# Gates of a hybrid diffusion layer: operand parts ahead of taking the product out of its bank

## The reference

```
h = rms_norm(x, norm1_w) * (1 + sc1) + sh1
proj = h @ w_in
hy, qkv, scv, gates = split(proj)
ya, yb, yc = hyena(hy), attention(qkv), short_conv(scv)
ga, gb, gc = split(gates, 3)            # 3 x 1024 columns
merged = sigmoid(ga)*(ya @ w_br_a) + sigmoid(gb)*(yb @ w_br_b) + sigmoid(gc)*(yc @ w_br_c)
x = x + g1 * (merged @ w_o)
```

## Time and profile before

| what | value |
|---|---|
| median of 3 executions | 2281.6 us (2279.53 to 2285.46) |
| the profiled execution's own time | 2278.91 us |
| its span, first to last instruction | 2277.1 us |
| mean granted TensorE clock | 0.975 |
| PE busy, share of the span | 94% |
| VectorE and ScalarE busy | 72% and 47% |
| gates of layer 0 | from 229.66 to 386.14 us |
| gates of layer 1 | from 1283.84 to 1440.26 us |

### The profile page before, as it was taken

The page is one execution under the profiler, slowest core; times in us unless marked ns, Lnnn a source line. Parts: engine busy times, 40 slices in busy tenths (PEclk is TensorE's granted clock), DMA queues, the critical chain, the costliest instruction groups (busy, mean ns, idle before and its releaser), DMA issues.

```text
span 2277.1 us, 34993 instructions
## 1 busy us (share of the span) xinstructions
PE 2138.9 (94%) x13094; PEld 1715.0 (75%) x13094; DVE 1630.9 (72%) x2405; ACT 1073.0 (47%) x1636; POOL 158.6 (7%) x176
## 2 busy tenths in 40 slices
PE   7998999999998997899998999999989999699999
PEld 2448999999656995566666999999765998466665
DVE  4857776654768646899997677663668654699997
ACT  2433444322712223788884444322451223588885
POOL 1010000000000100111110000000000100011110
PEclk8999999999999999899999999999999999799999
DMA  9772233212323423999993233322404431799997
GB/s 369 258 268 100 109 132 139 71 65 82 114 92 113 164 88 145 365 380 382 388 391 111 86 127 126 116 63 72 158 11 157 142 130 56 287 384 385 381 377 275
DMA packets 75656, 436.32 MB, mean 192 GB/s; under 512 B 8905, under 2 KB 9545, under 8 KB 34618
## 3 DMA queue, kind: packets, MB, share of 16 engines
q1 hardware_dynamic: 52896, 347.63, 39.7%
q0 software_dynamic: 18320, 72.87, 10.3%
q10 hardware_dynamic: 4300, 13.90, 1.8%
HBM read 384.87 MB, written 49.50 MB: 191 GB/s over the span
## 4 chain that ended last, share of the span: by engine, by line
PE 66%; DVE 15%; ACT 6%; issue 5%; DVEq 4%; DMA 3%; ACTq 0%; POOL 0%; POOLq 0%
PE ps L658 27%; PE ps L1173 9%; PE ps L1199 5%; PE ps L1177 4%; PE ps L831 3%; PE ps L885 3%; PE ps L1203 2%; DVE back L1918 2%; PE ps L757 2%; DVE front_r L1902 2%; PE ps L739 2%; PE ps L950 2%; ACT front_r L1267 2%; PE ps L697 1%; DVE back L1963 1%
## 5 line engine op out<-in xcount | busy, mean ns | idle before, releaser
L658 PE MATMUL ps<-front_r 128*128 128x320 f32 x3584 | 589.7, 311 | 12.2 <-DVE back_r L2194 8.4
L658 PEld LDWEIGHTS ps<-front_r 128*128 128x128 f32 x3584 | 542.3, 189 | 14.3 <-DVE front_r L1699 9.7
L1267 ACT ACTIVATE front_r<-ring 128x1024 fp32r<-128x1024 f32 (+1 forms) x204 | 184.9, 907 | 337.6 <-PE ps L658 256.0
L1267 ACT ACTIVATE back<-ps 128x512 f32<-128x512 f32 (+5 forms) x200 | 98.2, 507 | 375.1 <-PE ps L658 174.0
L1699 DVE TENSOR_TENSOR front_r<-ring,front_r 128x1024 fp32r<-128x1024 f32 x100 | 122.3, 1224 | 157.6 <-ACT front_r L1267 156.5
L885 PE MATMUL ps<-back_r,front_r 128*128 128x320 f32 x1152 | 176.7, 309 | 0.0
L885 PEld LDWEIGHTS ps<-back_r,front_r 128*128 128x128 f32 x1152 | 170.9, 188 | 0.0
L2288 DVE TENSOR_TENSOR back_r<-front,back_r 128x1024 fp32r<-128x1024 f32 x128 | 153.4, 1219 | 5.0 <-ACT back_r L1267 3.4
L1173 PE MATMUL ps<-back_r 128*80 128x512 f32 x384 | 152.0, 396 | 3.7 <-ACT back_r L1267 3.7
L1173 PE MATMUL ps<-back_r,front_r 128*80 128x512 f32 x384 | 151.9, 396 | 0.0
L658 PE MATMUL ps<-back_r,front_r 128*128 128x320 f32 x640 | 147.6, 312 | 0.0
(11 more groups left out here) (269 smaller groups left out, 3630.7 us busy)
## 6 DMA issues: line engine op xcount, KB each, us to landing
ring<-in_stream SPq DMA_DIRECT2D x186, 1024.0 KB, 6.5
front<-in_stream SPq DMA_DIRECT2D x80, 1024.0 KB, 18.0
back<-in_stream SPq DMA_DIRECT2D x48, 1024.0 KB, 18.9
gates<-back SPq DMA_DIRECT2D x24, 640.0 KB, 3.1
back<-gates POOLq DMA_DIRECT2D x48, 320.0 KB, 3.3
kspec<-back POOLq DMA_DIRECT2D x20, 512.0 KB, 7.0
front<-kspec POOLq DMA_DIRECT2D x4, 2048.0 KB, 10.8
rows<-front ACTq DMA_DIRECT2D x10, 520.0 KB, 2.7
```

Of the source, the lines that this page charges most:

```text
L658: mm = pe.matmul(tokh(b)[:, c0:c1], w(wp)[:, k, :], src(hp, k)[:, c0:c1], start=first, stop=last)
L1267: return act.activation(o, i, ACT.Copy)
```

## The change

In a step of the gates both engines turn round two pieces of work: the part of the operand of product n + 4 is made first, and product n is taken out of its bank second. What is waited for, the tiles, the banks and the instructions themselves are as before.

```
--- before.py
+++ after.py
@@ -1444,9 +1444,9 @@
                 operand_hi(2)
                 operand_hi(3)
                 for n in range(PRODUCTS):
-                    gate_taken(n)
                     if n + 4 < PRODUCTS:
                         operand_hi(n + 4)
+                    gate_taken(n)
                     if n == 7 * (N_GATE - 1):
                         act.wait_ge(qs_ready, l + 1)
                         act.activation(st5[:], st5[:], ACT.Sqrt, bias=eps[:, 0:1], scale=1.0 / HD).then_inc(qrt, 1)
@@ -2002,9 +2002,9 @@
                     operand_lo(n)
                 for n in range(PRODUCTS):
                     g, j = n // 7, n % 7
-                    gate_sum(n)
                     if n + 4 < PRODUCTS:
                         operand_lo(n + 4)
+                    gate_sum(n)
                     if j == 0:
                         weight_sum(g, 3)
                     elif j == 2 and g + 1 < N_GATE:
```

## The result

The changed kernel takes 2305.3 us (median of 4 executions, 2301.88 to 2306.52), the kernel before 2280.57 us beside it (2276.12 to 2285.46). The ratio is 1.0109, 95% interval 1.0095 to 1.0123. 2303.7 us was forecast. The change costs 24.7 us against the median beside it, where 22.1 us was forecast; that the two times lie only 1.6 us apart is in part luck, since the base stood 1.0 us lower this time. The profiled execution took 2305.6 us, its span is 2303.8 us.

The account below looks back on a forecast made before the run. PE was taken to bound the gates, apart from bank waits. Eleven waits of each kind, 1.77 us a pair, made each stage 167.5 us, the two 22.1 us longer: 2281.6 + 22.1 = 2303.7 us, range 2294 to 2312.

Parts of the forecast that it names:

- What bounds the gates: Gates: PE sets the pace at 1.76 us a product, losing 0.74 us a group waiting for VectorE to release bank 4.
- What the change takes away: Gates: VectorE's 1.87 us wait for the operand behind the sigmoid goes; alone, at most PE's 8.5 us a layer gained.
- The wait ahead of product 6: Gates, each group: product 6 waits 0.53 us for VectorE's sum of product 4, now behind an operand (4.05 against 3.52 us).
- The wait ahead of product 2: Gates, each group: product 2 newly waits 1.24 us for ScalarE's copy of product 0, through a chain across both engines.
- 12.32 + 0.53 + 1.24: Gates: group time without waits plus the waits ahead of products 6 and 2, giving 14.09 us a group, previously 13.06.
- the prediction's lower bound: Gates: if weight sum 2 held nobody, ScalarE would start 0.30 us earlier, 6.6 us less in all, 2297 us.
- Only the wait for bank 4: Rival, gates: the copy of product 0 is in time; 153.9 us a stage, 2276.4 us in all; chance 0.05.
- All waits gone: Rival, gates: no PE waits remain; 148.03 us a stage, 16.8 us less in all, 2264.8 us; chance 0.04.
- given back behind the stage: Rival, experts: DMA transfers start as early as now, so later computation recovers the gates' loss; 2281.6 us; chance 0.04.
- The fourth rival: Gates: the clock falls in the new gaps for a quarter of products, 59 us more, 2363 us; chance 0.03.
- settled into a cycle: Gates: the cycle repeats each group; a rival had waits growing instead, above 2312 us, chance 0.04.
- SP's store: SP's queue: gate store about 1.4 us later, next load not before some 13 us on; costed at nothing.

Follow-up runs that it names:

- ScalarE's half alone: Kernel before, with only ScalarE making the operand first and VectorE in its old order: 2264.82 us, ratio 0.9929.
- step 6 on ScalarE: Kernel before, with ScalarE making the operand first only in the step where the sigmoid L1426 stands: 2264.06 us, ratio 0.9933.
- The sum of product 4 first: Changed kernel, but VectorE sums product 4 ahead of the operand's low part, as before: 2308.59 us, ratio 1.0117.
- the copy first: Changed kernel, but ScalarE copies product 0 out of its bank ahead of the operand, as before: 2293.64 us, ratio 1.0054.
- the weight sum earlier: Changed kernel, but VectorE makes the next group's weight sum 2 ahead of the sum of product 5: 2297.96 us, ratio 1.0082.
- the sum of product 6 first: Changed kernel, but VectorE sums product 6 ahead of the operand's low part, as before: 2277.62 us, ratio 0.9986.
- VectorE's half without step 6: Kernel before, with only VectorE making the operand's low part first, except where it sums product 6: 2304.6 us, ratio 1.0108.

## Why the prediction was right, point by point

**What bounds the gates.** PE does, but for the release of a bank. Confirmed from the other side: with no wait (ScalarE's half alone) the stage is 148.14 us, and 148.03 was worked out from the pitch of 1.76 us.

**What the change takes away.** "The wait of 1.87 us goes": with ScalarE's half alone VectorE waits 0.17 us for that operand. In the changed kernel the wait doesn't go but is split: 0.76 us for the same operand (302.56), and 1.14 us for the next one (305.71), which is now the one behind the sigmoid. VectorE has caught up before the sum of product 4 even so: it waits 0.25 us for the operand ahead of that sum. One link of the change (step 6 on ScalarE) is worth 16 us, measured alone (2264.06 against 2280.2 us). The change had a gain in it, and gave it back and more.

**The wait ahead of product 6.** 0.53 us forecast, 0.53 measured, and the new cause as said: in the earlier trace rows the sum of product 4 was late because VectorE was behind, after the change because it stands behind a low part. The chain that ended last shows it, link by link, from the end of product 4's matmuls:

```profile
311.69 0.64 ACT front_r L1267
312.33 0.02 issue
312.36 0.69 DVE front_r L1902
...
313.14 0.50 DVE back L1918
313.64 0.04 issue
313.69 5.55 PE ps L885 x36
```

**The wait ahead of product 2.** 1.24 us forecast, 1.34 measured. From the start of product 6 (299.59, with the 0.10 by which its row is early) the links are: sum of product 5 at 1.12 (1.12 forecast), weight sum 2 at 1.53 (1.53), operand at 2.30 (2.26), low part at 2.97 (2.93), sum of product 6 at 3.75 (3.71), sigmoid at 4.27 (4.24), operand at 5.46 (5.41), copy from 5.99 to 6.41 (5.95 to 6.37). PE then went on 0.21 us after the copy had ended, not 0.15. These hundredths are the 0.10 us a group, 2.2 of the 2.8 us by which the stages came out longer than 167.5 each; another 0.28 in each layer is a single longer gap of ScalarE's, ahead of its operands at 333.70 and 1427.22 (0.45 us instead of 0.17).

**Where the working was right only in its sum.** The prediction added "12.32 + 0.53 + 1.24" as two costs. The sum of product 4 first shows that they aren't: the 14.19 us stay when the 0.53 are gone. The prediction's own links say so, had they been read to the end: product 5 stood "0.53 + 1.76" ahead of product 6, so whatever is taken from the 0.53 comes on top of the 1.24. What sets the group is one loop: from product 2 three products to the start of product 5, and from its end through both helpers (operand, low part, sum, weight sum, operand, low part, sum, sigmoid, operand, copy) back to the next product 2. Each link inside it counts in full or to the point where another takes over: the copy first takes 0.54 us off, the weight sum earlier 0.34 (the prediction's lower bound had 0.30 for this and 2297 us; 2297.96 was measured). The wait ahead of product 6 lies beside it, and costs only when the loop is broken, as with the sum of product 6 first.

**The rivals.** "Only the wait for bank 4" gave 153.9 us for a stage; the kernel that breaks the loop in step 6 has 154.07. "All waits gone" gave 2264.8 us; ScalarE's half alone has 2264.82. Both were the right price for a condition that the change as a whole doesn't meet. Nothing clear of the spread was given back behind the stage: the 24.85 us of the two stages are the 24.7 us of the medians. In the changed kernel's profile the clock stayed at 1.00 in both stages, with two pauses in each group and none longer than 1.39 us, so the rule of the Trainium skill on cycling through banks ("TensorE: Matmul & The Clock Gate", section "A second HAM failure mode: psum-queue depth-cycling") didn't come to bear on it. The fourth rival is not empty for all that: with the sum of product 4 first, and with VectorE's half without step 6, the clock fell once in one of the two stages, behind pauses of 1.92 and 1.77 us, and cost about 1.5 us each time. It was far from the quarter of all products that the rival's price supposed. The waits settled into a cycle at once: 14.18 and 14.19 us, group after group, but for the one longer gap of ScalarE's in each layer.

**SP's store.** Costed at nothing, with about 1.4 us of delay: the sigmoid ends 5.28 us after the start of product 6 instead of 3.86. The distance in the prediction was wrong, which changed nothing: the next load of SP's queue doesn't start some 13 us on but 6.0 us behind the store (316.08 and 310.03) before the change, and 5.8 us behind it (310.71 and 304.94) after it. In both kernels SP waits for PE there, and PE waits for no landing in any of the rows above.

## What to carry to other kernels

When two engines in line make an operand and also free the banks, ask of each turned pair which of the two pieces is waited for sooner. Here the operand is for four products ahead, while bank 4 is due again with one product in between: there VectorE has to take the product out first. The operand belongs in front where the other piece waits for somebody else (the sigmoid in step 6: 16 us from one pair of lines); in front of ScalarE's copy it cost nothing as long as VectorE kept its order. And look for the loop before adding up waits: taking away a wait that lies beside it gains nothing.

## What the runs showed of the hardware that was not expected

PE went on 0.21 us behind ScalarE's copy and 0.15 us behind VectorE's sum (306.00 to the 306.21 from which the next products count, and 305.96 to 306.11). Why these differ wasn't tried. ScalarE's longer gap, 0.45 us instead of 0.17, comes once in each layer (at 333.70 and 1427.22) and in no other group behind the sigmoid; its cause is open too.

The clock fell once in a stage in two of the eight other kernels, behind pauses of 1.92 and 1.77 us, and stayed full behind another pause of 1.92 us. What decides between these was not tried.
